# Streaming-encoder step with a 32-expert mixture: combine and bias matmuls moved to later gate_up blocks

## What is computed

```python
gu = (hb @ w_gate_up[e] + b_gate_up[e])        # 1024 -> 2048
gate, up = gu[:, :D_EXPERT], gu[:, D_EXPERT:]
gate = jnp.minimum(gate, SWIGLU_LIMIT)
up = jnp.clip(up, -SWIGLU_LIMIT, SWIGLU_LIMIT)
act = (up + 1.0) * (gate * jax.nn.sigmoid(SWIGLU_ALPHA * gate))
return act @ w_down[e] + b_down[e]             # 1024 -> 1024
```

## Time and profile before

| | |
|---|---|
| median of 3 runs | 1235.6 us (1233.99 to 1237.36) |
| the profiled execution | 1236.19 us; its span 1234.5 us |
| TensorE busy (matmuls) | 1185.0 us, 96% of the span |
| VectorE, ScalarE, GpSimd busy | 394.5, 224.3, 80.8 us |
| moved by DMA | 443.69 MB, mean 359 GB/s |
| granted TensorE clock, mean | 0.991 |

### The profile page before, as it was taken

One profiled execution on the slowest core, in us unless ns is written; L12 is line 12 of the kernel. 1 busy time (PEld: TensorE's weight loads), 2 busy tenths in 40 slices (PEclk: granted clock), 3 DMA queues, 4 the chain that ended last, 5 costly groups with the idle time before them and its releaser, 6 DMA issues.

```text
span 1234.5 us, 16076 instructions
## 1 busy us (share of the span) xinstructions
PE 1185.0 (96%) x6457; PEld 678.3 (55%) x6457; DVE 394.5 (32%) x647; ACT 224.3 (18%) x383; POOL 80.8 (7%) x242
## 2 busy tenths in 40 slices
PE   7999999999999999899998999999999998999996
PEld 6999999986435354344434343535535353553542
DVE  4648586756233423021212111111212111221222
ACT  4533672133101010000101010101101010110111
POOL 4100000010201001101100010101011010100000
PEclk9999999999999999899999999999999999999999
DMA  7453326588999999999999999999999999999994
GB/s 227 152 159 117 102 86 236 188 322 312 424 426 428 427 428 426 425 426 427 427 427 428 426 424 421 403 392 426 427 428 426 428 427 427 427 429 425 429 423 164
DMA packets 51854, 443.69 MB, mean 359 GB/s; under 512 B 4956, under 2 KB 5052, under 8 KB 23040
## 3 DMA queue, kind: packets, MB, share of 16 engines
q1 hardware_dynamic: 50512, 439.43, 86.3%
q0 software_dynamic: 1264, 3.20, 1.1%
HBM read 440.63 MB, written 1.98 MB: 359 GB/s over the span
## 4 chain that ended last, share of the span: by engine, by line
PE 81%; DMA 14%; issue 2%; DVE 1%; SPq 0%; ACT 0%; POOLq 0%; POOL 0%; DVEq 0%; ACTq 0%
PE ps L1602 27%; PE ps L1665 19%; DMA wexp<-in_w_gate_up_dram 11%; PE ps L1513 8%; PE ps L1258 7%; PE ps L1260 7%; PE ps L1259 7%; DMA wexp<-in_w_down_dram 2%; PE ps L1529 1%; PE ps L1563 1%; PE ps L1530 1%; PE ps L1617 1%; PE ps L1358 1%; DMA raw<-in_w_in_dram 1%; PE ps L1521 1%
## 5 line engine op out<-in xcount | busy, mean ns | idle before, releaser
L1602 PE MATMUL ps<-wexp,xt 128*64 128x512 f32 (+1 forms) x2368 | 475.9, 603 | 22.8 <-DMA wexp<-in_w_gate_up_dram 17.4
L1602 PEld LDWEIGHTS ps<-wexp,xt 128*64 128x64 f32 (+1 forms) x2368 | 154.2, 132 | 315.0 <-issue 314.5
L1665 PE MATMUL ps<-wexp,act_t 128*64 128x512 f32 (+1 forms) x1184 | 230.5, 593 | 5.9 <-issue 3.2
L1665 PEld LDWEIGHTS ps<-wexp,act_t 128*64 128x64 f32 (+1 forms) x1184 | 86.9, 131 | 136.6 <-issue 136.6
L1173 DVE TENSOR_TENSOR y<-y,ps 128x1024 f32<-128x1024 f32 x51 | 60.7, 1218 | 216.5 <-PE ps L1530 214.5
L758 ACT ACTIVATE g<-g 128x512 f32<-128x512 f32 x33 | 20.8, 630 | 553.8 <-DVE g L1187 553.8
L1258 PE MATMUL ps<-act_h,split 128*128 128x384 f32 x352 | 117.9, 335 | 0.0
L1260 PE MATMUL ps<-act_h,split 128*128 128x384 f32 x352 | 117.6, 334 | 0.0
L1259 PE MATMUL ps<-act_l,split 128*128 128x384 f32 x352 | 117.6, 334 | 0.0
L1513 PEld LDWEIGHTS ps<-pick,xn 128*128 128x128 f32 x768 | 91.1, 196 | 14.7 <-issue 14.7
L1513 PE MATMUL ps<-pick,xn 128*128 128x128 f32 x768 | 94.1, 283 | 1.7 <-POOL pick L536 1.7
(11 more groups left out here) (305 smaller groups left out, 814.1 us busy)
## 6 DMA issues: line engine op xcount, KB each, us to landing
wexp<-in_w_gate_up_dram SPq DMA_DIRECT2D x106, 2048.0 KB, 22.0
wexp<-in_w_down_dram SPq DMA_DIRECT2D x52, 2048.0 KB, 24.0
wexp<-in_w_gate_up_dram SPq DMA_DIRECT2D x44, 1024.0 KB, 18.2
wexp<-in_w_down_dram SPq DMA_DIRECT2D x22, 1024.0 KB, 9.2
raw<-in_w_in_dram SPq DMA_DIRECT2D x20, 1024.0 KB, 5.1
raw<-in_w_proj_a_dram SPq DMA_DIRECT2D x4, 1024.0 KB, 5.5
raw<-in_w_out_dram SPq DMA_DIRECT2D x4, 1024.0 KB, 5.0
raw<-in_w_proj_b_dram SPq DMA_DIRECT2D x2, 1024.0 KB, 6.5
```

The costliest lines, as they stand in the source:

```text
L1602: i_ = pe.matmul(ps[s0:s0 + w, b, :], xt[:, k, s0:s0 + w], wexp[place(k, x) % RINGS][:, at_:at_ + UC], start=k == 0, stop=k == CB - 1)
L1665: i_ = pe.matmul(ps[s0:s0 + w, 6 + c, :], act_, wexp[place(CB + m, x) % RINGS][:, D * kk + UC * c:D * kk + UC * c + UC], start=k == 0, sto ...
```

## The change

In passes 2 to 16 the combine of tiles 0 and 1 moves from behind block 1 to behind block 4, the bias from behind block 0 to behind block 5, and the combine of tile 2 from behind block 3 to behind block 6. Pass 1 (`first`) and pass 17 (`last`) stay. No instruction is added or taken out, and no other engine's code is touched.

```diff
-                    if k == 0:
+                    if k == (0 if first or last else 5):
                         pe.wait_ge(sel_ready, it + 1)
...
-                    if k == 1:
+                    if k == (1 if first or last else 4):
                         add_up(it, first, (0, 1))
-                    if k == 3:
+                    if k == (3 if first or last else 6):
                         add_up(it, first, (2,))
```

## The result

The changed kernel takes 1257.67 us (median of 4 runs, 1257.37 to 1258.54) against 1235.61 before: 22.1 us slower, ratio 1.0186 (95% interval 1.0170 to 1.0201). The forecast was 1254.2 us, between 1246 and 1261. Its profiled execution took 1258.54 us, 22.35 over the one of before.

The account below looks back on a forecast made before the run. DMA and TensorE both stand near their limit, the DMA setting the pace from pass 6. TensorE 24.0 us late, less 3.6 spare, 1.5 and 0.3, gives +18.6 on 1236.2, so 1254.8; median 1254.2 us, range 1246 to 1261.

Parts of the forecast that it names:

- The wait for VectorE: Passes 2 and 3: tables end later, so TensorE's transposes wait for VectorE's last product, +4.8 us in each pass.
- The clock: TensorE's clock slows behind idle time: 1.0 us each in passes 2 and 3, 2.0 in pass 4, +4.0 together.
- the gather's delay: Pass 4: the chain from tile 2's combine through VectorE's table and GpSimd to the gather moves by +10.4 us.
- the spare of 3.6: Behind down block 1 of pass 4: the issue of loads may slip 3.6 us before the DMA idles.
- SyncE's late first load: First load of pass 5: issued about 508 us, using 20 us of 8.9 spare; 13 us late alone, contained in 20.4.
- the transfer at 805 us: Pair of loads read as finding the queue empty: 5.5 us for 1 MB, hence 8.0 us for an unqueued 2 MB.
- the thin stretch: Around passes 9 and 10 the DMA moves 409 and 408 GB/s over 110 us against 427: 4.9 us lost.
- the last two terms: Earlier releases of slots win -1.5 us around passes 9 and 10; pass 8 into passes 9 and 10 gives -0.3.
- rival C: Later passes: work behind the last landing is paid in up to six waits, +8.4 us, 1262.6 us; 10 in 100.
- +18.6: Forecast loss in us for the whole kernel, on an execution of 1236.2 us, giving 1254.8.
- A: Rival: with the DMA full, the delay of passes 2 to 4 is not felt; 1231 to 1234 us; 8 in 100.
- B: Rival: activations of passes 2 and 3 come in time, only pass 4 counts, +7.0 us, 1242.6 us; 8 in 100.

Follow-up runs that it names:

- passes 2 and 3 alone: Kernel before, with combines and bias in their new places in passes 2 and 3 only: 1246.95 us, ratio 1.0103.
- the clock kernel: Changed kernel plus 17 small matmuls of zeros in passes 2 and 3, filling TensorE's two waits for the activations: 1252.78 us, ratio to before 1.0141.
- passes 2 to 4 alone: Kernel before, with combines and bias in their new places in passes 2 to 4 only: 1255.06 us, ratio 1.0165.

## Why the prediction held

**Passes 2 and 3: right in kind, one term too small.** The wait for VectorE: +4.8 each forecast, 4.7 measured (counted from the start of the pass, the down projection starts 5.3 us later; 0.6 of that is clock). The clock: 1.0 each forecast, 2.8 measured: 0.6 on transposes and token gates, 2.2 on the down projection. I had argued that most of the slow time falls on small work. It lasted into the down projection. Each pass is 7.6 us longer, not 5.8.

**Pass 4: right in kind, the gather's delay too large.** The delay was to be 10.4 us, with some 12 us of waiting; the gather waits 9.5. The delay is 22.4 less the 14.9 by which TensorE enters the pass late, so 7.5; the last section says where 3 us went. The clock took 2.1 us (2.0 forecast).

**Lateness and spare.** TensorE 24.0 us late at down block 1 forecast, 24.6 measured; the spare of 3.6 leaves 20.4 forecast, 20.6 measured. That it came so close is luck: passes 2 and 3 took 3.5 us more than forecast, mostly clock, and pass 4 took 2.8 less, by its shorter path to the gather. SyncE's late first load (510.0 us, 22.3 later) lands 13.2 us late, as forecast, and was contained in this. Two readings of the forecast were loose: the transfer at 805 us did not find the queue empty (the load issued at 801.9 us landed at 807.5), though its 8.0 us for 2 MB came out; and the thin stretch around passes 9 and 10 had lost 4.8 us, not 4.9.

**What failed: the last two terms, -1.5 and -0.3 us, and a part of the spare.** From the landing at 536 us to the end the DMA gets 1.8 us later instead of 1.8 earlier. The first 1.1 of it come right behind the empty queue. The second transfer of that pair lands at 542.1 us, 5.9 behind the first, where such landings are otherwise 4.9 apart, and the delay stays: the last landing of pass 6's gate_up is at 620.8 us instead of 599.1, so 21.7 late. The spare was worth 2.9 us of TensorE's 24.6, not 3.6. The rest comes behind pass 8. The windows over passes 9 and 10, against the earlier trace rows:

```profile
772.00:827.00 55.00, 54.74 (x280) 25.91 (x278) 10.53 (x17) 6.16 (x13) 3.66 (x12) 1.00 1.00 404
827.00:882.00 55.00, 54.73 (x279) 25.98 (x277) 11.12 (x17) 5.15 (x12) 3.66 (x12) 1.00 0.99 411
```

409 and 408 GB/s became 404 and 411: the earlier releases bought nothing. In pass 8 TensorE no longer waits for blocks 6 and 7, but for block 4, and both combines and the bias, 4.3 us, now follow that landing. It reaches pass 9 at 771.7 us, 23.7 late, where the DMA was 21.6 late. That is rival C's mechanism, paid once for 2 us and not in every pass. The pair of profiles understates it: from the last weights of pass 8 to the last gate_up weights of pass 11 the trace of before takes 152.3 us, but the eight others that keep the bias and tiles 0 and 1 in their old places in these passes take 149.9 to 151.0, and the four with the new places 151.5 to 153.2. So the late passes cost about 2 us in that stretch, where 1.8 were to be won. The two misses, 2.5 and 1.1 us, make up 3.6 of the 3.7 between +18.6 and +22.35.

**The rivals.** A needed 24 us of queue; 20.6 of TensorE's 24.6 us reached the DMA. B (only pass 4 counts) is refuted: passes 2 and 3 alone cost 1.0%. C's mechanism holds once, as said, and not for the 8.4 us that it was priced at.

The Trainium skill's fit ("DMA: Bandwidth & Descriptors", on the anatomy of one DMA; 6.8 us as an estimate for an unqueued 2 MB) stands against landings of 7.6 to 8.1 us here. The page gives it for transfers that GpSimd issues through software descriptors, and these loads go out by SyncE's hardware queue, so the fit was carried over further than the page goes. The Trainium skill's advice ("Perfetto Trace Analysis", on identifying the most-contended engine), as the prediction read it, named the DMA. The runs show that its share of busy time does not tell how much lateness of another engine it can take.

## What to carry to other kernels

Before moving work within an engine's order, look at what the other engines do between its old place and the next point where the first engine needs them: here a queue of table work had been covered by four blocks, and one was left. Where a DMA queue is full, its time from issue to landing, less the unqueued time, is the lateness that the kernel forgives; it differs from transfer to transfer, and it held here within 1 us (3.6 read, 2.9 found). Work with no consumer nearby, like these tables, goes ahead of work that waits for the engine whose order is to be changed.

## What was not expected of the hardware

The dynamic loop between passes 4 and 5 runs only through its branches, and its time hangs on whether the DMA queue has run dry. SyncE's instructions at L430 and L429 (first and last start), before and after:

```profile
L430 SPq COMPARE_BRANCH  x3: 50/50/58, 479.9 to 485.9; - x3
...
L429 SPq ALU_OP  x3: 33/33/43, 484.8 to 486.2; - x3
```

```profile
L430 SPq COMPARE_BRANCH  x3: 50/50/58, 505.2 to 508.3; - x3
...
L429 SPq ALU_OP  x3: 33/33/43, 507.1 to 508.5; - x3
```

From the first branch to its target 4.9 us went by before, and 1.9 after. Before, the transfers then in the queue took another 20 us to land; after, 1 us. The other traces say the same, counted at that branch: 4.5 to 4.8 us in the nine with 7 to 22 us of transfers queued, 2.5 with 2 us (the clock kernel) and 1.8 with 1 us (passes 2 to 4 alone). GpSimd's own gap there goes from 2.7 to 0.4 us.

The Trainium skill ("Runtime: NRT & Kernel Launch", on instruction fetch mechanics) says that a taken branch may need its target fetched by DMA. The traces fit. The DMA's queues in the gap (packets, MB, share of 16 engines), before, from 480.0 to 482.9 us and from 482.9 to 484.8:

```profile
q1 hardware_dynamic: 83, 1.26, 102.2%
```

```profile
q1 hardware_dynamic: 57, 0.77, 97.6%
q14 instruction: 2, 0.02, 2.3%
```

and after, from 505.2 to 506.3 us:

```profile
q14 instruction: 2, 0.02, 5.5%
q1 hardware_dynamic: 1, 0.00, 0.1%
```

The same two instruction packets move in both, but before they move only some 3 us behind the branch, while the DMA is full of weights. They don't wait for the whole queue: the gap is no longer with 22 us queued than with 7. That the packets on this queue are those of SyncE's target is my reading. In the changed kernel GpSimd's path from the tables to the gather takes 7.4 us instead of 10.2, so nearly 3 us came back exactly where the queue had run dry.
